# Refilling the expert ring in order, and gathering four channels two chunks later

## The chip, the cores and the metric

One NeuronCore of a Trainium2 chip runs the kernel. The metric is the device time of one execution in microseconds; lower is better.

## The reference

The kernel computes one layer of a hybrid decoder on 256 tokens of width 1024, in float32. The first half is `h = h + W_o(sum of three gated mixers of RMSNorm(h))` (sparse attention, causal pooling, short convolution). The second half, where the change lies, is a mixture of 32 experts in 4 groups of 8; each token goes to the two best experts of its best group:

```python
top_v, top_i = lax.top_k(e_in, EXPERT_TOP_K)              # best 2 of the 8 in the best group
top_w = jax.nn.softmax(top_v, axis=-1) * g_prob[tok, g_sel][:, None]
for e in range(N_EXPERTS):                                # w1, w3: 1024x256, w2: 256x1024
    h = jax.nn.silu(xt @ w1[e]) * (xt @ w3[e])
    out = out + combine[:, e:e + 1] * (h @ w2[e])
```

A final RMSNorm follows. The expert weights are 96 of the 132 MiB that the kernel reads, and every one is read once.

## The kernel before

**Blocks and chunks.** Experts are worked four at a time, as 8 blocks. An expert gets at most 32 tokens in a pass, so a block is 4 experts of 32 token places. The weights of a block come as 12 chunks of 1 MiB: 8 chunks `q` = 0 to 7 hold w1 and w3 for one eighth of the input channels (128) each, 4 chunks hold w2 for a quarter of the output columns each. A *round* is 4 blocks, 48 chunks (`NC`), numbered `c` = 0 to 47; there are two rounds in a pass, and with these inputs one pass.

**The ring.** Chunks land in 25 slots of 1 MiB (`ring`). `AT[c]` (line 78) is the slot of chunk c: 0 to 24 go to slots 0 to 24, chunk 25 to slot 0, chunks 26 to 47 to slots 2 to 23. Slots 1 and 24 thus hold one chunk in a round, the others two. `earlier(c)` is the chunk that held the slot before c: 25 back for chunk 25, 24 back for chunks 26 to 47. In the second round chunks 0 and 2 to 23 follow chunks that lie 23 and 24 back.

**SyncE's queue** issues every weight load, in chunk order. Chunks 0 to 23 are issued early, as slots come free from the first half of the layer (`early`, lines 551 to 625). Line 626 waits for `passes_done`, then line 627 loads chunk 24 (slot 24 held the router's constants and small tiles until then). Lines 629 to 631 load chunks 25 to 29 singly, 632 to 639 the rest of the round (two chunks in one transfer; the last one in halves), 643 to 664 the second round. Each of these first waits until TensorE has counted the slot's earlier chunk as used (`expert_used`).

**The router.** TensorE counts the tokens of each expert and signals `count_full` (line 1773). VectorE turns the counts into the number of passes in five small steps with the tile `pcnt`, and signals `passes_done` (lines 1330 to 1337). TensorE gathers channels 0 to 3 of block 0 (lines 1807 to 1813), then waits for `passes_done`, reads the number and enters the loop.

**TensorE in a block** (lines 1818 to 1906). `gather(k)` multiplies a slice of 128 channels of `h` with the 0/1 matrix `sel`, which leaves the block's tokens in PSUM bank 2. Channels 4 to 7 are gathered inside the block that uses them, 4 and 5 ahead of chunk q = 1, 6 and 7 ahead of q = 2. VectorE copies all four to `xgT`, with the norm's gain (line 1360, `xg1_done`); TensorE waits for that ahead of q = 4. After q = 2 come transposes of the weights of the block's tokens, from which VectorE makes `rslot`, `cmbT` and `share` (1364 to 1366, `cmb_done`) and then the next block's `sel` (1341). VectorE works in that order: 1360, 1364 to 1366, 1341, 1349. Channels 0 to 3 of the next block are gathered after q = 7 and between the second products; in the last block of a round (j = 3) they follow q = 4, 5, 6 and 7 one by one, each behind a wait for the next `sel` (1848 to 1850). Then come the second products (`second`) and the sums into the output banks (`combine`).

**After the last block** the sums are normed and stored by ScalarE, VectorE and SyncE. The tiles `fin`, `fing` and two of squares lie over ring slots 12 to 15.

Of the kernel before, what the change touches and what calls it, by code (L numbers as in the profile page):

```python
# [13 lines left out]
P = 128  # L14
D = 1024
T = 256
# [23 lines left out]
CAP = 32  # L40
EB = P // CAP
NB = NE // EB
EPS = 1e-6
NEG = -1e30
SLOT = 2048
SLOTS = 25

# [27 lines left out]
SLOT_XLO, SLOT_MERGED, SLOT_O, SLOT_XHI = 18, 19, 20, 21  # L75
SLOT_ATT, SLOT_Q, SLOT_ROUTER = 22, 23, 24

AT = [*range(SLOTS), 0, *range(2, SLOTS - 1)]
CHUNK_SET = {n: (SET_A, SET_B)[i % 2] for i, n in enumerate(SPLITS)}

NQ1 = KT
NQ2 = NQT
NQ = NQ1 + NQ2
ROUND = 4
NC = ROUND * NQ
ECHUNK = EB * 2 * HID
MAXPASS = T // CAP
# [4 lines left out]
def turn(c):  # L94

    return HELD[AT[c]].index(c)
# [15 lines left out]

K_ID = 0
K_IOTA = K_ID + P

K_TRI = K_IOTA + CAP
K_ONE = K_TRI + P
K_SL = K_ONE + P
K_RK = K_SL + HEADS
K_FOLD = K_RK + PER_GROUP  # L120
K_CAP = K_FOLD + 32
K_FOLD2 = K_CAP + MAXPASS
K_CB = K_FOLD2 + RC

K_DIST = K_CB + NT * HEADS * 16
# [9 lines left out]
def build(nc, x, params, consts, front, projs, small, wgrp, vecs, routerw, routerb, experts, out):  # L135
    with ExitStack() as ctx:
# [35 lines left out]
        def router(name, shape):  # L172

            t = over(name, shape, "ring", in_router[0])
            in_router[0] += math.prod(shape[1:])
            return t
# [3 lines left out]
        rb = router("rb", [P, RC])  # L180
        sPT1 = router("sPT1", [P, 3 * P])
        wg = router("wg", [P, 2, P])
        pcnt = router("pcnt", [P, 8 + MAXPASS])
        hidT = sb("hidT", [P, 4, KVG, 32])
        cw2 = sb("cw2", [P, 4, HD])
        kcT = over("kcT", [P, 32], "ring", SLOT_ATT * SLOT + 15 * P)
# [55 lines left out]

        routed = sb("routed", [P, 2, NT, NE])
        comb, rank = routed[:, 0], routed[:, 1]
        mask = over("mask", [P, NT, NE], "ring", in_router[0] - 8 - MAXPASS - 2 * P)[:]


        fin = over("fin", [P, NT, D], "ring", 12 * SLOT)
        fing = over("fing", [P, D], "ring", 13 * SLOT)
        last_squares = over("last_squares", [P, NT, D], "ring", 14 * SLOT)  # L250
        act_squares = over("act_squares", [P, NT, D], "ring", 15 * SLOT)
        xgT = kv[:].rearrange("p (k s) -> p k s", k=KT)
        yN, ylo = over("yN", [P, 2 * QC], "gab"), over("ylo", [P, 2 * QC], "gab", 2 * QC)
        gflat = gab[:].rearrange("p a c -> p (a c)")
# [7 lines left out]
        lg, gap1, key1, left, gap2, key2 = [kv[:, i * NT * RC:(i + 1) * NT * RC] for i in range(6)]  # L262
        first, second_of, both = [gflat[:, i * NT * RC:(i + 1) * NT * RC] for i in range(3)]
        top1, big1, top2, big2, behind, e2, weight, c1, c2, total = [vflat[:, 256 + 16 * i:256 + 16 * i + NT * ROWS] for i in range(10)]
        gexp = vflat[:, 416:432].rearrange("p (t e) -> p t e", t=NT)
        share1, share2 = [vflat[:, i * NT * NE:(i + 1) * NT * NE].rearrange("p (t e) -> p t e", t=NT) for i in range(2)]
        cmbT = over("cmbT", [P, T], "vbd")[:]
# [14 lines left out]
        rk8 = conr[:, K_RK - K_TRI:K_RK + PER_GROUP - K_TRI]  # L282
        fold = conr[:, K_FOLD - K_TRI:K_FOLD + 32 - K_TRI]
        fold2 = conr[:, K_FOLD2 - K_TRI:K_FOLD2 + RC - K_TRI]
        steps_of_cap = conr[:, K_CAP - K_TRI:K_CAP + MAXPASS - K_TRI]

# [213 lines left out]
        SCATTERED = (3, 5, 6, 7, 7)  # L502


        def summed(t, qt):

            c = t * QC if qt > 1 else qt * QC
            return bank[4 + t if qt < 2 else 4 + qt][:, c:c + QC]
# [9 lines left out]
        def _(sp):  # L518
# [104 lines left out]
            sp.wait_ge(wo_full, 4)  # L623
            early(SET_B + 2, SLOT_MERGED)
            early(SLOT_XHI, SLOT_ATT)
            sp.wait_ge(passes_done, 1)
            sp.dma_start(ring[:, SLOT_ROUTER], single(SLOT_ROUTER)).then_inc(router_slot_in, 16)

            for c in range(SLOTS, SLOTS + SINGLES):
                sp.wait_ge(expert_used, GIVEN + earlier(c) + 1)  # L630
                sp.dma_start(ring[:, AT[c]], single(c)).then_inc(expert_in[AT[c] // 2] if c % 2 else single_in, 16)
            for c in range(SLOTS + SINGLES, NC - 2, 2):
                sp.wait_ge(expert_used, GIVEN + earlier(c + 1) + 1)
                sp.dma_start(slots_of(c), experts[c // NQ, c % NQ // 2]).then_inc(expert_in[AT[c] // 2], 16)
            half = ECHUNK // 2
            for c, f, sem_in in ((NC - 2, slice(0, ECHUNK), expert_in[AT[NC - 2] // 2]), (NC - 1, slice(0, half), last_half_in),
                                 (NC - 1, slice(half, ECHUNK), last_in)):
                sp.wait_ge(expert_used, GIVEN + earlier(c) + 1)
                sp.dma_start(ring[:, AT[c], f], single(c)[:, f]).then_inc(sem_in, 16)
# [3 lines left out]
            with sp.Fori(1, passes * (NB // ROUND)) as r:  # L643
                def pair(c):

                    sp.wait_ge(expert_used, r * NC + (GIVEN + max(earlier(c), earlier(c + 1)) + 1))
                    sp.dma_start(slots_of(c), rounds[bass.ds(r % (NB // ROUND), 1), c // NQ, c % NQ // 2]  # L647
                                 .rearrange("o p c -> (o p) c")).then_inc(expert_in[AT[c] // 2], 16)

                for c in range(0, SLOT_ROUTER, 2):  # L650
                    pair(c)
                for c, sem_in in ((SLOT_ROUTER, router_slot_in), (SLOTS, expert_in[0])):
                    o = c % 2 * ECHUNK
                    sp.wait_ge(expert_used, r * NC + (GIVEN + earlier(c) + 1))
                    sp.dma_start(ring[:, AT[c]], rounds[bass.ds(r % (NB // ROUND), 1), c // NQ, c % NQ // 2, :, o:o + ECHUNK]
                                 .rearrange("o p c -> (o p) c")).then_inc(sem_in, 16)
                for c in range(SLOTS + 1, NC - 2, 2):
                    pair(c)
                for c, f, sem_in in ((NC - 2, slice(0, ECHUNK), expert_in[AT[NC - 2] // 2]), (NC - 1, slice(0, half), last_half_in),
                                     (NC - 1, slice(half, ECHUNK), last_in)):  # L660
                    sp.wait_ge(expert_used, r * NC + (GIVEN + earlier(c) + 1))
                    o = c % 2 * ECHUNK
                    sp.dma_start(ring[:, AT[c], f], rounds[bass.ds(r % (NB // ROUND), 1), c // NQ, c % NQ // 2, :, o + f.start:o + f.stop]
                                 .rearrange("o p c -> (o p) c")).then_inc(sem_in, 16)
# [765 lines left out]
        def _(pe):  # L1430
# [354 lines left out]
            def have_expert(bb, j, q):  # L1785

                c = j * NQ + q
                if SLOTS <= c < SLOTS + SINGLES and c % 2 == 0:
                    pe.wait_ge(single_in, 16 * (SINGLES // 2))
                if c == NC - 1:  # L1790
                    pe.wait_ge(last_in, bb * 16 + 16)
                elif c == SLOT_ROUTER:
                    pe.wait_ge(router_slot_in, bb * 16 + 16)
                else:
                    pe.wait_ge(expert_in[AT[c] // 2], bb * 32 + 16 * (turn(c) + 2))


            def gather(*ks):
# [7 lines left out]

            pe.wait_ge(sel_step, 1)
            for k in range(4):
                for t in range(NT):
                    ins = mm(bank[2 + k // 2][:, (k % 2) * P:(k % 2 + 1) * P], h[:, t, k * P:(k + 1) * P],  # L1810
                             flat(sel[:, t]), start=(t == 0), stop=(t == NT - 1))
                if k % 2:
                    ins.then_inc(xg_full, 1)

            pe.wait_ge(passes_done, 1)
            passes = pe.value_load(npass[0:1, 0:1], min_val=1, max_val=MAXPASS)

            def round_of_blocks(bb, last):

                for j in range(ROUND):  # L1820
                    b = bb * ROUND + j
                    pe.wait_ge(hn_done, b + 1)
                    for q in range(NQ1):
                        if q in (1, 2):
                            gather(2 * q + 2, 2 * q + 3)
                        if q == 0:
                            pe.wait_ge(xg0_done, b + 1)
                        if q == 2:
                            pe.wait_ge(xg1_done, b + 1)
                        if q == 4:  # L1830
                            pe.wait_ge(xg1_done, b + 2)
                        have_expert(bb, j, q)
                        for e in range(EB):
                            ins = mm(bank[0][CAP * e:CAP * (e + 1)], xgT[:, q, CAP * e:CAP * (e + 1)],  # L1834
                                     expert(j, q, e), start=(q == 0), stop=(q == NQ1 - 1))
                        if q == NQ1 - 1:
                            ins.then_inc(hid1_full, 1)
                        else:
                            ins.then_inc(expert_used, 1)
                        if q == 2:  # L1840
                            pe.wait_ge(sel_done, b + 1)
                            pe.wait_ge(hT_done, b + 1)
                            for t in range(NT):
                                nc.tensor.transpose(bank[1][:, t * P:(t + 1) * P], flat(selw[:, t]), ident)
                            for t in range(NT):
                                ins = mm(bank[1][:, T:T + 1], flat(sel[:, t]), stat[:, 26 + t:27 + t], start=(t == 0), stop=(t == NT - 1))
                            ins.then_inc(cmb_full, 1)
                        if j == ROUND - 1 and q >= 4:
                            pe.wait_ge(sel_step, b + 2)
                            gather(q - 4)  # L1850
# [184 lines left out]
```

## Time and profile before

| | us |
|---|---|
| median of 3 runs | 416.36 |
| lowest, highest | 415.26, 416.62 |
| the profiled execution | 415.54 |
| its span in the profile | 413.7 |

The span is what the profiler sees of the execution; 1.8 us lie around it. TensorE is busy for 382.1 us of the span (92%), VectorE for 198.4, ScalarE for 149.0. The DMA engines moved 139.89 MB. All times in the rows below are microseconds from the start of the span.

### The profile page before, as it was taken

Reading aid. Unit: us, or ns where it says so; the run is one execution under the profiler, and the core shown is the slowest. Engines: PE = TensorE matmul, PEld = TensorE weight load, DVE = VectorE, ACT = ScalarE, POOL = GpSimd, SP = SyncE. Lnnn points to the kernel's source line nnn. Section 1 sums busy time; section 2 is a strip of 40 time slices with the busy share of each in tenths; the row PEclk is TensorE's granted clock in tenths of the full one; section 3 lists DMA queues with packets and bytes.
Section 4 is the critical chain, followed back from the end, with each engine's and each line's share of the span. In section 5 each row is a group of like instructions: output and inputs, shape, how many; then the busy total and the mean of one; then the engine's idle time right before and its main releaser. Section 6 shows DMA issues by size and latency. Waiting matters only on the chain.

```text
span 413.7 us, 7503 instructions
## 1 busy us (share of the span) xinstructions
PE 382.1 (92%) x2990; PEld 265.2 (64%) x2990; DVE 198.4 (48%) x392; ACT 149.0 (36%) x283; POOL 12.2 (3%) x34
## 2 busy tenths in 40 slices
PE   7999999999999999999989999999899998688582
PEld 5999988767777777788865555555355544245241
DVE  3838693999898775784263121212122221211215
ACT  6834451638565635442221222222222222112023
POOL 3000000300000000000011000000000000000001
PEclk9999999999999999999999999999999999879996
DMA  7999999643441587569998999999999999999982
GB/s 299 412 412 358 395 390 365 265 152 101 154 147 67 196 329 281 184 243 398 420 418 321 394 428 429 426 414 430 426 425 428 426 417 429 428 428 428 425 335 103
DMA packets 17599, 139.89 MB, mean 338 GB/s; under 512 B 2336, under 2 KB 2720, under 8 KB 5792
## 3 DMA queue, kind: packets, MB, share of 16 engines
q1 hardware_dynamic: 16704, 138.60, 83.5%
q10 hardware_dynamic: 864, 0.84, 0.6%
q8 instruction: 24, 0.39, 0.4%
q14 instruction: 7, 0.06, 0.0%
HBM read 138.38 MB, written 1.05 MB: 337 GB/s over the span
## 4 chain that ended last, share of the span: by engine, by line
PE 73%; DMA 13%; DVE 6%; SPq 4%; ACT 2%; issue 2%; POOL 0%; POOLq 0%; DVEq 0%; ACTq 0%
DMA ring<-in_experts 12%; PE bank L1834 10%; PE bank L1802 6%; PE bank L1874 6%; PE bank L1596 5%; PE bank L1598 4%; PE bank L1597 4%; PE bank L1454 4%; PE bank L1455 4%; PE bank L1456 4%; SPq L647 4%; PE bank L1886 3%; PE bank L1718 2%; PE bank L1719 2%; PE bank L1717 2%
## 5 line engine op out<-in xcount | busy, mean ns | idle before, releaser
L1834 PE MATMUL bank<-ring,kv 128*32 128x512 f32 x512 | 65.7, 619 | 10.1 <-DMA ring<-in_experts 8.9
L481 DVE TENSOR_TENSOR part<-ring,part 128x2048 fp32r<-128x2048 f32 (+1 forms) x26 | 57.8, 2231 | 17.1 <-ACT part L474 17.1
L474 ACT CAST part<-ring 128x2048 fp32r<-128x2048 f32 (+1 forms) x26 | 48.0, 1847 | 29.5 <-DMA ring<-in_front 29.4
L1802 PEld LDWEIGHTS bank<-qcur,h 128*128 128x128 f32 x256 | 31.7, 191 | 28.2 <-issue 27.3
L1376 DVE SCALAR_TENSOR_TENSOR ylo<-bank,stat,yN 128x256 fp32r<-128x256 f32 (+1 forms) x40 | 17.1, 430 | 54.1 <-ACT yN L952 34.1
L1596 PE MATMUL bank<-part,xhi 128*128 128x512 f32 x96 | 39.2, 408 | 0.0
L1802 PE MATMUL bank<-qcur,h 128*128 128x128 f32 x256 | 39.1, 289 | 0.0
L1874 PE MATMUL bank<-ring,hidT 128*32 128x256 f32 (+1 forms) x640 | 35.2, 342 | 3.9 <-DMA ring<-in_experts 3.4
L1598 PE MATMUL bank<-part,xlo 128*128 128x512 f32 x96 | 37.6, 391 | 0.0
L1597 PE MATMUL bank<-part,xhi 128*128 128x512 f32 x96 | 37.5, 391 | 0.0
L1454 PE MATMUL bank<-xhi,part 128*128 128x256 f32 x128 | 36.6, 286 | 0.5 <-DVE xlo L1021 0.5
L1455 PE MATMUL bank<-xlo,part 128*128 128x256 f32 x128 | 36.2, 283 | 0.0
L1456 PE MATMUL bank<-xhi,part 128*128 128x256 f32 x128 | 36.2, 283 | 0.0
L1834 PEld LDWEIGHTS bank<-ring,kv 128*32 128x32 f32 x512 | 13.0, 110 | 32.0 <-issue 23.6
L952 ACT ACTIVATE yN<-bank,stat 128x256 fp32r<-128x256 f32 (+1 forms) x40 | 17.2, 431 | 42.3 <-PE bank L1874 42.3
L944 ACT ACT_TABLE_LOAD x7 | 9.0, 1283 | 50.6 <-DVE stat L1366 50.6
L1886 PE MATMUL bank<-yN,cmbT 128*128 128x256 f32 (+1 forms) x80 | 23.4, 318 | 2.8 <-DVE ylo L1376 2.5
L1454 PEld LDWEIGHTS bank<-xhi,part 128*128 128x128 f32 x128 | 24.5, 192 | 1.7 <-DVE xlo L1021 0.9
L1874 PEld LDWEIGHTS bank<-ring,hidT 128*32 128x32 f32 x640 | 16.6, 109 | 13.6 <-ACT hidT L946 3.1
L1455 PEld LDWEIGHTS bank<-xlo,part 128*128 128x128 f32 x128 | 24.6, 192 | 0.0
L1456 PEld LDWEIGHTS bank<-xhi,part 128*128 128x128 f32 x128 | 24.6, 192 | 0.0
L1360 DVE TENSOR_TENSOR kv<-bank,prm 128x512 f32<-128x512 f32 x8 | 5.5, 692 | 39.7 <-PE bank L1802 39.7
(251 smaller groups left out, 586.9 us busy)
## 6 DMA issues: line engine op xcount, KB each, us to landing
ring<-in_experts SPq DMA_DIRECT2D x30, 2048.0 KB, 33.5
ring<-in_experts SPq DMA_DIRECT2D x34, 1024.0 KB, 8.4
ring<-in_front SPq DMA_DIRECT2D x28, 1024.0 KB, 5.4
ring<-in_front SPq DMA_DIRECT2D x4, 512.0 KB, 6.8
ring<-in_projs SPq DMA_DIRECT2D x4, 512.0 KB, 5.2
ring<-in_experts SPq DMA_DIRECT2D x4, 512.0 KB, 32.5
ring<-in_front SPq DMA_DIRECT2D x2, 560.0 KB, 9.4
h<-in_x SPq DMA_DIRECT2D x2, 512.0 KB, 3.8
```

The lines of the kernel that those rows point to most:

```text
L474: nc.scalar.copy(high(n, half)[:, 0:c].bitcast(F32R), raw(n, half)[:, 0:c]).then_inc(hi_done, 1)
L481: nc.vector.tensor_tensor(low(n, half)[:, 0:c].bitcast(F32R), raw(n, half)[:, 0:c], high(n, half)[:, 0:c], ALU.subtract).then_inc(split_do ...
L1454: mm(dst, whi, ahi, start=start, stop=False)
L1455: mm(dst, whi, alo, start=False, stop=False)
L1456: return mm(dst, wlo, ahi, start=False, stop=stop)
L1596: mm(bank[t][:], XH[:, kk, cols], whi[:, k], start=(kk == 0), stop=False)
L1597: mm(bank[t][:], XH[:, kk, cols], wlo[:, k], start=False, stop=False)
L1598: ins = mm(bank[t][:], XL[:, kk, cols], whi[:, k], start=False, stop=(kk == KT - 1))
L1802: ins = mm(bank[2][:, (k % 4) * P:(k % 4 + 1) * P], h[:, t, k * P:(k + 1) * P], flat(sel[:, t]), start=(t == 0), stop=(t == NT - 1))
L1834: ins = mm(bank[0][CAP * e:CAP * (e + 1)], xgT[:, q, CAP * e:CAP * (e + 1)], expert(j, q, e), start=(q == 0), stop=(q == NQ1 - 1))
L1874: ins = mm(second_out(p, slice(CAP * e, CAP * (e + 1))), hT[:, ht, CAP * e:CAP * (e + 1)], second_weights(j, p, ht, e), start=(ht == 0), s ...
L1886: mm(sum_of_piece(t, p), onehot, yN[:, place(p)].bitcast(F32R), start=False, stop=False)
```

## The change

It does four things.

1. Chunks 25 to 47 take slots 0 to 22 in order. Every one of them now follows a chunk 25 back. In the second round chunks 0 to 22 follow chunks 23 back, and 23 and 24 have slots that held one chunk. The semaphores of arrival are renumbered (`arrival`). A pair of the second round waits for the later of its two.
2. Chunk 24's load waits for `count_full` in place of `passes_done`. `pcnt` and the constants `K_CAP` leave slot 24; `fin` and its companions move down by one slot.
3. Channels 4 and 5 are gathered ahead of q = 3, channels 6 and 7 ahead of q = 4.
4. TensorE waits for `passes_done` and reads the number ahead of its gather of channel 3, in place of after it.

```diff
-AT = [*range(SLOTS), 0, *range(2, SLOTS - 1)]
+AT = [*range(SLOTS), *range(ROUND * NQ - SLOTS)]
...
-        pcnt = router("pcnt", [P, 8 + MAXPASS])
+        pcnt = vflat[:, 432:440 + MAXPASS]
...
-        fin = over("fin", [P, NT, D], "ring", 12 * SLOT)
+        fin = over("fin", [P, NT, D], "ring", 11 * SLOT)
...
-        steps_of_cap = conr[:, K_CAP - K_TRI:K_CAP + MAXPASS - K_TRI]
+        steps_of_cap = con[:, K_CAP:K_CAP + MAXPASS]
...
+        def arrival(c):
+            return expert_in[c % SLOT_ROUTER // 2]
...
-            sp.wait_ge(passes_done, 1)
+            sp.wait_ge(count_full, 1)
             sp.dma_start(ring[:, SLOT_ROUTER], single(SLOT_ROUTER)).then_inc(router_slot_in, 16)
...
-                sp.dma_start(ring[:, AT[c]], single(c)).then_inc(expert_in[AT[c] // 2] if c % 2 else single_in, 16)
+                sp.dma_start(ring[:, AT[c]], single(c)).then_inc(arrival(c) if c % 2 else single_in, 16)
...
             for k in range(4):
+                if k == 3:
+                    pe.wait_ge(passes_done, 1)
+                    passes = pe.value_load(npass[0:1, 0:1], min_val=1, max_val=MAXPASS)
                 for t in range(NT):
...
-            pe.wait_ge(passes_done, 1)
-            passes = pe.value_load(npass[0:1, 0:1], min_val=1, max_val=MAXPASS)
...
-                        if q in (1, 2):
-                            gather(2 * q + 2, 2 * q + 3)
+                        if q in (3, 4):
+                            gather(2 * q - 2, 2 * q - 1)
```

## Rows read from the trace of the kernel before

**Rows 1.** The page, what the DMA engines moved in 40 slices of 10.34 us.

```profile
GB/s 299 412 412 358 395 390 365 265 152 101 154 147 67 196 329 281 184 243 398 420 418 321 394 428 429 426 414 430 426 425 428 426 417 429 428 428 428 425 335 103
```

**Rows 2.** The chain that ended last, 150 to 414: start, us, what.

```profile
348.27 49.81 DMA ring<-in_experts
398.21 1.10 PE bank L1874 x16
```

**Rows 3.** Stretches: from:to, us, TensorE's granted clock, DMA share, GB/s.

```profile
212.00:218.00 6.00, 1.00 1.01 422
218.00:221.00 3.00, 1.00 0.88 279
...
224.50:227.50 3.00, 1.00 0.75 243
227.50:234.00 6.50, 1.00 0.95 369
218.00:234.00 16.00, 1.00 0.91 335
264.00:396.00 132.00, 0.97 1.01 425
```

**Rows 4.** SyncE's timeline, chunks 24, 25 and 26: start, us, line.

```profile
218.03 0.33 SPq L627 DMA_DIRECT2D ring<-in_experts  x1
...
220.43 0.33 SPq L631 DMA_DIRECT2D ring<-in_experts  x1
...
224.60 0.33 SPq L631 DMA_DIRECT2D ring<-in_experts  x1
```

**Rows 5.** Timeline from 211 to 226, router and block 0: start, us, engine, line.

```profile
216.28 0.61 PE L1772 MATMUL bank<-mask,conr 128*128 128x32 f32 x4
...
217.83 0.18 DVE L1337 CAST npass<-pcnt 128x2 int32<-128x2 f32 x1
...
223.58 0.69 DVE L1360 TENSOR_TENSOR kv<-bank,prm 128x512 f32<-128x512 f32 x1 [3.59 <-PE bank L1802]
```

**Rows 6.** TensorE's read of the pass count: ns min/median/max, start.

```profile
L1816 PEldq TENSOR_LOAD <-npass x1: 490/490/490, 218.0 to 218.0; - x1
```

**Rows 7.** The chain, 150 to 414, where it runs along TensorE: start, us, what.

```profile
216.95 2.05 PE bank L1810 x16
219.31 1.07 PE bank L1834 x8
220.37 1.09 PE bank L1802 x8
...
282.41 1.07 PE bank L1834 x8
...
305.16 1.06 PE bank L1834 x8
```

**Rows 8.** Timeline of blocks 6 and 7: start, us, idle before and releaser.

```profile
363.37 1.93 PE L1834 MATMUL bank<-ring,kv 128*32 128x512 f32 x8 [2.01 <-DMA ring<-in_experts]
...
378.41 1.07 PE L1834 MATMUL bank<-ring,kv 128*32 128x512 f32 x8
...
383.07 1.06 PE L1834 MATMUL bank<-ring,kv 128*32 128x512 f32 x8 [0.43 <-DMA ring<-in_experts]
...
384.89 0.16 DVE L1364 COPY stat<-bank 128x1 f32<-128x1 f32 x1 [1.51 <-PE bank L1846]
...
385.84 0.42 DVE L1341 TENSOR_TENSOR qcur<-con,routed 128x256 f32<-128x256 f32 x1
...
388.39 1.07 PE L1834 MATMUL bank<-ring,kv 128*32 128x512 f32 x8 [2.55 <-DMA ring<-in_experts]
...
393.20 1.06 PE L1834 MATMUL bank<-ring,kv 128*32 128x512 f32 x8 [1.46 <-DMA ring<-in_experts]
```

**Rows 9.** Stretches of blocks 6 and 7: busy times, then granted clock, DMA share, GB/s.

```profile
360.00:364.00 4.00, 1.99 (x12) 0.20 (x8) 0.00 (x0) 0.00 (x0) 0.00 (x0) 0.50 0.99 422
...
384.00:388.00 4.00, 1.84 (x18) 0.85 (x14) 1.77 (x6) 0.00 (x0) 0.00 (x0) 1.00 0.99 422
```

More of the change, by code:

```diff
@@ L44 @@
 NEG = -1e30
+NQ1 = KT
+NQ2 = NQT
+NQ = NQ1 + NQ2
+ROUND = 4
 SLOT = 2048
@@ L76 @@
 SLOT_ATT, SLOT_Q, SLOT_ROUTER = 22, 23, 24
-AT = [*range(SLOTS), 0, *range(2, SLOTS - 1)]
+AT = [*range(SLOTS), *range(ROUND * NQ - SLOTS)]
 CHUNK_SET = {n: (SET_A, SET_B)[i % 2] for i, n in enumerate(SPLITS)}
[L83 to L86, printed above, removed]
 NC = ROUND * NQ
@@ L114 @@
 K_IOTA = K_ID + P
-K_TRI = K_IOTA + CAP
+K_CAP = K_IOTA + CAP
+K_TRI = K_CAP + T // CAP
 K_ONE = K_TRI + P
@@ L120 @@
 K_FOLD = K_RK + PER_GROUP
-K_CAP = K_FOLD + 32
-K_FOLD2 = K_CAP + MAXPASS
+K_FOLD2 = K_FOLD + 32
 K_CB = K_FOLD2 + RC
@@ L244, in build @@
         comb, rank = routed[:, 0], routed[:, 1]
-        mask = over("mask", [P, NT, NE], "ring", in_router[0] - 8 - MAXPASS - 2 * P)[:]
-        fin = over("fin", [P, NT, D], "ring", 12 * SLOT)
-        fing = over("fing", [P, D], "ring", 13 * SLOT)
-        last_squares = over("last_squares", [P, NT, D], "ring", 14 * SLOT)
-        act_squares = over("act_squares", [P, NT, D], "ring", 15 * SLOT)
+        mask = over("mask", [P, NT, NE], "ring", in_router[0] - 2 * P)[:]
+        fin = over("fin", [P, NT, D], "ring", 11 * SLOT)
+        fing = over("fing", [P, D], "ring", 12 * SLOT)
+        last_squares = over("last_squares", [P, NT, D], "ring", 13 * SLOT)
+        act_squares = over("act_squares", [P, NT, D], "ring", 14 * SLOT)
         xgT = kv[:].rearrange("p (k s) -> p k s", k=KT)
@@ L630, in _ @@
                 sp.wait_ge(expert_used, GIVEN + earlier(c) + 1)
-                sp.dma_start(ring[:, AT[c]], single(c)).then_inc(expert_in[AT[c] // 2] if c % 2 else single_in, 16)
+                sp.dma_start(ring[:, AT[c]], single(c)).then_inc(arrival(c) if c % 2 else single_in, 16)
             for c in range(SLOTS + SINGLES, NC - 2, 2):
                 sp.wait_ge(expert_used, GIVEN + earlier(c + 1) + 1)
-                sp.dma_start(slots_of(c), experts[c // NQ, c % NQ // 2]).then_inc(expert_in[AT[c] // 2], 16)
+                sp.dma_start(slots_of(c), experts[c // NQ, c % NQ // 2]).then_inc(arrival(c), 16)
             half = ECHUNK // 2
-            for c, f, sem_in in ((NC - 2, slice(0, ECHUNK), expert_in[AT[NC - 2] // 2]), (NC - 1, slice(0, half), last_half_in),
+            for c, f, sem_in in ((NC - 2, slice(0, ECHUNK), arrival(NC - 2)), (NC - 1, slice(0, half), last_half_in),
                                  (NC - 1, slice(half, ECHUNK), last_in)):
@@ L647, in pair @@
                     sp.dma_start(slots_of(c), rounds[bass.ds(r % (NB // ROUND), 1), c // NQ, c % NQ // 2]
-                                 .rearrange("o p c -> (o p) c")).then_inc(expert_in[AT[c] // 2], 16)
+                                 .rearrange("o p c -> (o p) c")).then_inc(arrival(c), 16)
                 for c in range(0, SLOT_ROUTER, 2):
                     pair(c)
-                for c, sem_in in ((SLOT_ROUTER, router_slot_in), (SLOTS, expert_in[0])):
+                for c, sem_in in ((SLOT_ROUTER, router_slot_in), (SLOTS, arrival(SLOTS))):
                     o = c % 2 * ECHUNK
@@ L658, in _ @@
                     pair(c)
-                for c, f, sem_in in ((NC - 2, slice(0, ECHUNK), expert_in[AT[NC - 2] // 2]), (NC - 1, slice(0, half), last_half_in),
+                for c, f, sem_in in ((NC - 2, slice(0, ECHUNK), arrival(NC - 2)), (NC - 1, slice(0, half), last_half_in),
                                      (NC - 1, slice(half, ECHUNK), last_in)):
@@ L1794, in have_expert @@
                 else:
-                    pe.wait_ge(expert_in[AT[c] // 2], bb * 32 + 16 * (turn(c) + 2))
+                    pe.wait_ge(arrival(c), bb * 32 + 16 * (turn(c) + 2))
             def gather(*ks):
```

## The prediction, made before the changed kernel was run

> **What bounds the kernel now.** I read the chain that ended last first. Its late part is one transfer of expert weights: issued at 348.27, landed 49.81 us later, and within 0.2 us of the landing TensorE starts the products that needed it [rows 2]. So the weights' arrival sets the end, and the last 8 us or so of work hang on it. A transfer that is 50 us under way says that the queue is deep. Next the page's row of GB/s: from the slice that starts at 238 us on it is flat near 425, up to the last two slices [rows 1]; over 264 to 396 it is 425 [rows 3]. In that stretch nothing on an engine can make the weights come earlier; the reader should look for what is lost before it. The row shows a dip of 321 in the slice from 217 to 227 us, between 418 and 394 [rows 1]. In narrower stretches: 422 up to 218, then 279, later 243, then 369 until 234; over 218 to 234 the mean is 335 [rows 3]. That is (1 - 335/425) x 16 = 3.4 us of lost transfer time. Every us of it that is won back brings all later weights 1 us earlier, as long as TensorE keeps up.
>
> Two holes make most of it. The first, (1 - 279/425) x 3 = 1.0 us, is around chunk 24: SyncE issues it at 218.03, as soon as the pass count is written at 218.01 [rows 4, 5], and the earlier transfers run out at about 218.5. The second, (1 - 243/425) x 3 = 1.3 us, is around chunk 26: chunk 25 is issued at 220.43, when q = 0 of block 0 ends, and chunk 26 only at 224.60 [rows 4], since its slot is that of chunk 2, and the two pairs of gathers stand ahead of chunk 2. After 227.5 another (1 - 369/425) x 6.5 = 0.9 us is lost while single chunks trickle out.
>
> **The change part by part.** The sum is made against the profiled execution, 415.54 us, which is 0.8 under the median of 416.36; I give the result for both.
>
> *Chunk 24.* `count_full` comes with the end of the count's products, 216.28 + 0.61 = 216.89, the pass count at 217.83 + 0.18 = 218.01 [rows 5]: 1.1 us earlier, while the DMA engines still run at 422 [rows 3]. The first hole closes. But chunk 24 then moves from about 218.5 to 221.0 (1.05 MB at 425 GB/s is 2.5 us), and chunk 25 still waits for q = 0 of block 0.
>
> *The read of the pass count.* It took 0.49 us on TensorE's queue, from 218.0 on, while the array was busy with gathers until 219.0 [rows 6, 7]. Ahead of channel 3 it finds fewer products in front of it (three quarters of 2.05 us, done at 218.5), so that gather starts some 0.3 us late; what then follows it, the loop's entry, is partly behind the gather. Between 0 and 0.5 us on the start of block 0, I take 0.2. So chunk 25 is issued at about 220.6, close to the end of chunk 24's data. In the second hole the issue at 224.60 came about as late against the end of the data as this one would, or slightly later: I take 0.9 of its 1.3 us for the new hole at chunk 25 (bounds 0.3 and 1.3).
>
> *Chunks 26 to 29.* Chunk 26 follows chunk 1 now, and no gather stands ahead of q = 1. With 1.0 us for a chunk of products (219.31 to 220.37) and 1.1 for a pair of gathers [rows 7], q = 1 ends at 221.5 and q = 2 at 222.5: chunks 26 and 27 are issued then, 3.1 us and more ahead of 224.60. The second hole goes. Chunk 28 follows q = 3, which has the transposes (0.7) and the gather of channels 4 and 5 ahead: about 225.3. Chunk 29 follows q = 4, at about 228.4. By then 5 chunks of 2.5 us have been issued, enough until 234. Of the 0.9 us lost after 227.5 I take half as won (bounds none and all).
>
> *Sum for the weights.* Lost before 3.4. Lost after: 0.9 at chunk 25, 0.4 to 0.5 later, together 1.4. Gain 2.0 us. Highest: all 3.4. Lowest: the second hole goes (1.3), the first (1.0) goes, and a full hole of 1.3 opens at chunk 25: 1.0.
>
> The Trainium skill (DMA: Bandwidth & Descriptors, section Anatomy of one DMA) puts a fixed 2.0 us on a transfer, mostly the wait for the receipt of the last byte, which the next transfer in a queue does not pay. It gives it for GpSimd's queue. By it a late chunk costs the engines less than 2 us, and the two holes of 1.0 and 1.3 agree.
>
> *The gathers' place in the block.* Nothing is added: 16 products of 128 x 128 and VectorE's copy of 0.69 us [rows 5] stand as before. But the copy's cover goes. Before, q = 2, the transposes and q = 3 lay between gathers and wait, over 2.7 us; now the gather of 6 and 7 is directly followed by the wait. VectorE's copy of block 0 starts at 223.58, within 0.1 of the end of the gathers (two chunks at 1.07 and 1.0 and two gathers at 1.1, from 219.31 [rows 7]); it takes 0.69, and I give the answer another 0.1: 0.9 us a block, 8 blocks, 7.2 us of TensorE. Bounds: 0.7 (the copy alone) and 1.5. In the last block of a round the wait for the next `sel` after q = 4 comes on top: VectorE needs 384.89 to 386.26 = 1.4 us from `rslot` to `sel` [rows 8], and q = 4 covers 1.0: 0.4 more. The SiLU's wait for `cmb_done` stays covered by q = 5 to 7 (3 us).
>
> *Does TensorE keep up?* Before, three blocks took 282.41 - 219.31 = 63.1 and the fourth 22.7 [rows 7], and the weights caught up with TensorE in block 5 to 7. Blocks with 0.9 more, the fourth with 1.3, start from 219.5: block 4 at 309.4, block 5 at 331.3, block 6 at 353.2, block 7 at 375.1. Block 7 began at 378.41 before [rows 8], held by weights; 2.0 us earlier is 376.4. So TensorE is 1.3 us ahead even there. In block 7, with weights 2.0 earlier: q = 2 at 381.1 (383.07 before), transposes done at 382.8, gather, q = 3 and gather until 386.0, wait 0.9, q = 4 at 386.9 (its weights come at 386.4), the wait for `sel` until 388.1, gather, q = 5, gather until 390.4; the weights of q = 6 come at 391.2 (393.20 before). From there all is as before, 2.0 us earlier. The 7.2 us lie in waits for weights, among them 2.55, 2.01 and 1.46 [rows 8]; the thinnest cover is this 0.8 us.
>
> *Order of the slots later on.* A chunk of the second round waits for one chunk more of use, some 2 us, and for TensorE's lag of 3 to 8 us. Against this stands a queue of up to 50 us [rows 2]. Nothing. Renumbered semaphores, the moved tiles and constants: same instructions, nothing.
>
> **Forecast:** 415.54 - 2.0 = 413.5 for the profiled execution, 414.4 beside the median.
>
> **The rivals.**
> A, the hole only moves: the engines stand idle at chunk 25 as long as at 24 and 26, or block 0 starts 0.5 later. Gain 0.3 to 1.2 us, about 415.5. For it: chunk 25's issue hangs on q = 0 alone. Against: chunk 24's issue moves less than the hole at 26 was wide.
> B, all is won: 3.0 to 3.4 us, about 413.1. Chunk 25 would have to be issued while 24 flows well.
> C, the clock falls late. In block 6 the granted clock was 0.50, the 1.2 GHz level, from 360 to 364, around a wait of 2.01 us, and 8 products took 1.93 us in place of 1.06 [rows 8, 9]; this was covered by waits for weights. In block 7 it stayed at 1.00, though TensorE was busy for 1.84 of 4 us [rows 9]. The change moves the gathers out of the wait ahead of q = 2 of block 7, so that TensorE idles some 2.7 us there. If the clock then is at the lower level over the last 7 us, which nothing covers, half of them is lost: +3.5 - 2.0 = +1.5, about 417.9. It decides if the drop reaches past the landing of the last pair.
> The Trainium skill (TensorE: Matmul & The Clock Gate, Part 1) says that the gate goes by how busy the array has been; these rows fit it in block 6 and leave block 7 open.
> D, the gather's wait becomes the bound: if it costs x a block, the cover of 1.3 + 2.7 us up to q = 2 of block 7 is gone at x = 1.5, the gain at x = 1.75, and from 1.9 the kernel is slower by over 0.3%; at 2.2 it would be at 420. Against: VectorE has nothing else to do there.
> E, no effect: the weights are bound somewhere that I don't see. 416.4.
>
> **The numbers.** What can be told from no change is 0.3%, 1.25 us. Forecast 0.53 (own range 413.8 to 415.1), B 0.05: faster 0.58. A 0.25, E 0.05: same 0.30. C 0.07, D 0.05: slower 0.12. The range goes from B's lower end, 416.4 - 3.4 = 413.0, to 416.6, 0.2 above E.
>
> **What would show it.** After the change: chunk 24 issued near 217.0, 26 and 27 before 223; 218 to 234 at 385 to 395 GB/s in place of 335; the chain still on a transfer, landing near 396; eight waits of TensorE of about 0.9 us behind line 1360. It is wrong if the last landing has not moved, if the chain's end runs along TensorE from block to block, or if the clock is below 1 after 390.

## The result and the profile after

The changed kernel took 412.56 us in the median of 8 executions (411.73 to 414.75), the kernel before 415.56 (8 executions, 415.24 to 416.62). The ratio is 0.9934, 95% interval 0.9909 to 0.9959: 2.7 us less. The profiled execution took 412.76 us (span 411.0) against 415.54: 2.8 less. Among the 8 executions, three took 414.46 to 414.75, the others 411.73 to 412.76. I had forecast 2.0 less and, from a median of 416.36 over three executions of the kernel before, the range 413.0 to 416.6. The time is below it.

The stretches of the changed kernel (from:to, us, granted clock, DMA share, GB/s), to be read beside [rows 3]:

```profile
218.00:221.00 3.00, 1.00 0.99 391
221.00:224.50 3.50, 1.00 0.86 286
224.50:227.50 3.00, 1.00 1.01 429
227.50:234.00 6.50, 1.00 1.01 426
218.00:234.00 16.00, 1.00 0.97 389
...
264.00:378.00 114.00, 1.00 1.01 428
```

The holes at chunks 24 and 26 and the thin supply after 227.5 have gone, one hole at chunk 25 has come. Over 218 to 234 the mean is 389 in place of 335. The last row is the surprise: over 264 to 378 the rate is 428. The kernel before, in the same stretch:

```profile
264.00:378.00 114.00, 0.97 1.01 425
```

SyncE's timeline in block 0, chunks 24 to 28 (start, us, line), beside [rows 4]:

```profile
217.10 0.33 SPq L632 DMA_DIRECT2D ring<-in_experts  x1
...
220.85 0.33 SPq L636 DMA_DIRECT2D ring<-in_experts  x1
...
221.71 0.33 SPq L636 DMA_DIRECT2D ring<-in_experts  x1
...
222.57 0.33 SPq L636 DMA_DIRECT2D ring<-in_experts  x1
...
225.27 0.33 SPq L636 DMA_DIRECT2D ring<-in_experts  x1
```

TensorE's waits from 180 us on (who waited for whom: us in total, times, longest):

```profile
PE bank L1839 <- DVE kv L1365: 6.3, 8, 0.8
...
PE bank L1839 <- DMA ring<-in_experts: 2.8, 1, 2.8
```

Line 1365 is VectorE's copy of channels 4 to 7 (1360 before). Its eight waits are there, 0.8 us each. In their place the waits for weights ahead of the first products have shrunk to one, of 2.8 us. That one is in block 7, and the chain that ended last goes through it (start, us, what):

```profile
332.83 46.68 DMA ring<-in_experts
...
379.64 1.06 PE bank L1839 x8
```

The weights of q = 2 of block 7 land 3.4 us earlier (383.07 in [rows 8], 379.64 here). But behind them the chain runs along TensorE, and no later transfer of weights is on it. TensorE's timeline shows why (start, us, line, idle before):

```profile
374.95 1.92 PE L1839 MATMUL bank<-ring,kv 128*32 128x512 f32 x16
379.64 1.06 PE L1839 MATMUL bank<-ring,kv 128*32 128x512 f32 x8 [2.77 <-DMA ring<-in_experts]
...
381.28 2.03 PE L1807 MATMUL bank<-qcur,h 128*128 128x128 f32 x8
383.23 1.78 PE L1839 MATMUL bank<-ring,kv 128*32 128x512 f32 x8
384.95 1.16 PE L1807 MATMUL bank<-qcur,h 128*128 128x128 f32 x8
386.89 1.07 PE L1839 MATMUL bank<-ring,kv 128*32 128x512 f32 x8 [0.78 <-DVE kv L1365]
```

After the idle 2.77 us a pair of gathers takes 2.03 us instead of 1.16 and the products of q = 3 take 1.78 instead of 1.07: the clock is at its lower level. The same in the stretches (busy times, granted clock, DMA share, GB/s):

```profile
380.00:384.00 4.00, 4.00 (x26) 2.57 (x22) 0.00 (x0) 0.00 (x0) 0.00 (x0) 0.67 1.02 434
384.00:388.00 4.00, 3.17 (x24) 1.12 (x16) 1.82 (x6) 0.00 (x0) 0.00 (x0) 0.91 0.99 422
```

So two things differed from my account: the weights gained 3.4 us, not 2.0, and 0.6 us of that (3.4 - 2.8) was lost again in block 7.

### The profile page after: what moved, and what is told of

It is laid out like the page before. It is cut to its first block, busy times and chain, and to the rows that moved or that the text cites. A ratio compares the mean times of both kernels' runs of the same rounds, so it can differ in the third digit from the quotient of the medians.

```text
span 411.0 us, 7504 instructions
## 1 busy us (share of the span) xinstructions
PE 379.0 (92%) x2990; PEld 265.8 (65%) x2990; DVE 197.1 (48%) x392; ACT 149.0 (36%) x283; POOL 13.1 (3%) x34
## 4 chain that ended last, share of the span: by engine, by line
PE 75%; DMA 12%; DVE 7%; ACT 2%; issue 2%; POOL 0%; POOLq 0%; SPq 0%; DVEq 0%; ACTq 0%
DMA ring<-in_experts 11%; PE bank L1839 11%; PE bank L1807 6%; PE bank L1879 6%; PE bank L1601 5%; PE bank L1602 4%; PE bank L1603 4%; PE bank L1459 4%; PE bank L1460 4%; PE bank L1461 4%; PE bank L1891 3%; PE bank L1722 2%; PE bank L1724 2%; PE bank L1723 2%; PE bank L1563 1%
## 5 line engine op out<-in xcount | busy, mean ns | idle before, releaser
L1839 PE MATMUL bank<-ring,kv 128*32 128x512 f32 x512 | 62.1, 604 | 10.0 <-DVE kv L1365 6.3
L1807 PEld LDWEIGHTS bank<-qcur,h 128*128 128x128 f32 x256 | 32.6, 195 | 21.9 <-issue 19.9
L1839 PEld LDWEIGHTS bank<-ring,kv 128*32 128x32 f32 x512 | 14.1, 109 | 34.5 <-issue 24.2
```

Source lines behind the costliest of these rows:

```text
L1807: ins = mm(bank[2][:, (k % 4) * P:(k % 4 + 1) * P], h[:, t, k * P:(k + 1) * P], flat(sel[:, t]), start=(t == 0), stop=(t == NT - 1))
```

## The experiments

The theory at the start: the gain is the closed holes in block 0; the gathers' place costs TensorE 0.8 to 0.9 us a block, covered until block 7, where the clock can fall. The rival: the gathers' place is what makes the gain, or the order of the slots raises the flat rate. All ratios are against the kernel before in the same series, whose median was 415.4 to 415.9. "Less" or "slower" beside a ratio is worked out from it; where two changed kernels are compared, it is by their medians.

**e1**, the changed kernel with the gathers back:

```diff
-                        if q in (3, 4):
-                            gather(2 * q - 2, 2 * q - 1)
+                        if q in (1, 2):
+                            gather(2 * q + 2, 2 * q + 3)
```

> The changed kernel with the gathers of channels 4 to 7 back ahead of q = 1 and 2; slots in order, chunk 24 at the count and the early read stay. Theory 1 (the gain is the weights' holes in block 0; the gathers' new place costs TensorE 0.9 us a block, hidden up to block 7, and there an idle stretch of 2.8 us ahead of q = 2 after which the clock falls in some executions): chunk 26 is issued about 1 us later than in the changed kernel, at 222.9, still in time, so the holes stay as small (218 to 234 near 385 GB/s). No wait behind the copy of channels 4 to 7, no long idle stretch ahead of q = 2 of the last block: 411.5 to 412.5 us, ratio to before 0.991 to 0.993, all executions together, none at 414.5. Theory 2 (the gathers' move is what brings chunks 26 to 28 early enough): 218 to 234 falls back to about 360 GB/s and the time is 414 or more.

412.84 us, ratio 0.9931 (0.9918 to 0.9945), five executions within 412.49 to 413.32. The rate over 218 to 234 was 360, which is what the second theory had said, but its time (414 or more) was not. So the gathers' move does help the weights, by (389 - 360)/428 x 16 = 1.1 us. Of the changed kernel's 11 executions (3 of them in e14 below), the five with a mean clock of 0.995 (median 411.85) are 1.0 us below e1's median and the five with 0.985 or 0.986 (median 414.49) 1.6 above, so in the mean over all of them nothing is left of the gain. No execution of e1 was near 414.5.

**e2**, gathers back in blocks 3 and 7 alone:

```diff
-                        if q in (3, 4):
+                        if j == ROUND - 1 and q in (1, 2):
+                            gather(2 * q + 2, 2 * q + 3)
+                        if j < ROUND - 1 and q in (3, 4):
                             gather(2 * q - 2, 2 * q - 1)
```

> The changed kernel, but in the last block of each round (blocks 3 and 7) the gathers stand ahead of q = 1 and 2 as before; in the other six blocks they stay ahead of q = 3 and 4. Theory 1 (in block 7 TensorE idles ahead of q = 2 and in some executions runs at the lower clock afterwards, with nothing to cover it): that idle stretch is filled with 2.2 us of gathers, the clock stays at 1.00 from 380 on, and the executions near 414.5 go: all at 411 to 412.5, ratio 0.990 to 0.992. Theory 2 (the spread from 411.7 to 414.7 comes from somewhere else, such as the front of the kernel): the same two groups of times as in the changed kernel.

412.07 us, ratio 0.9912 (0.9898 to 0.9925), all five within 411.62 to 412.64. The group near 414.5 is gone, as theory 1 said; the chain ends on the landing of the last pair again. One number of mine was wrong: the clock did not stay at 1.00. In e2's profile it was 1.00 over 380 to 384 and fell behind the next wait, the 2.08 us ahead of q = 4 (busy times, granted clock, DMA share, GB/s; then TensorE):

```profile
384.00:388.00 4.00, 2.94 (x12) 1.16 (x12) 0.00 (x0) 0.00 (x0) 0.00 (x0) 0.58 0.99 422
```

```profile
385.06 1.94 PE L1841 MATMUL bank<-ring,kv 128*32 128x512 f32 x8 [2.08 <-DMA ring<-in_experts]
```

There it cost nothing: TensorE still waited for the last weights afterwards. Filling the wait ahead of q = 2 thus did not keep the clock up to the end, it moved the fall to a place where it is covered.

**e3**, slots in order and nothing else (the diff of `AT`, `arrival` and the moved `fin`, on the kernel before):

> The kernel before with slots 0 to 22 refilled in order, and nothing else of the change: chunk 24 still waits for the pass count, gathers ahead of q = 1 and 2. Theory 1: chunk 26 is issued when q = 1 ends, at about 222.5 in place of 224.6, and chunks 27 to 31 one chunk of use earlier; the hole at chunk 24 (1.0 us) stays, the one at chunk 26 (1.3 us) and most of the 0.9 us behind it go: 2.0 us less, about 413.6, ratio 0.995. Rival (the order of the slots raises the flat rate after 264 from 424 to 428 GB/s, which is worth another 1 us): ratio 0.993, and 427 or more GB/s over 264 to 378.

414.44 us, ratio 0.9971 (0.9959 to 0.9983): 1.2 us less. 218 to 234 at 373 GB/s, from 264 at 425. The order of the slots closes holes ((373 - 335)/425 x 16 = 1.4 us) and does not touch the flat rate.

**e4**, chunk 24 at the count and nothing else (on the kernel before, with `pcnt` and `K_CAP` moved; the cut shows two places of the edit):

```diff
-K_TRI = K_IOTA + CAP
+K_CAP = K_IOTA + CAP
+K_TRI = K_CAP + T // CAP
...
-            sp.wait_ge(passes_done, 1)
+            sp.wait_ge(count_full, 1)
             sp.dma_start(ring[:, SLOT_ROUTER], single(SLOT_ROUTER)).then_inc(router_slot_in, 16)
```

> The kernel before with chunk 24 issued at the count of tokens instead of at the pass count (and the tile and constants that this needs moved out of its slot), and nothing else of the change. Theory 1: chunk 24 is issued at 217.0, the hole around 219 closes, but the next hole opens at chunk 25 (issued at 220.4, when chunk 24's data ends at 221) and the one at chunk 26 stays: gain 0.1 to 0.6 us, ratio 0.9985 to 1.0. Rival (each hole stands for itself and closing one is worth its 1.0 us): ratio 0.9975. The flat rate after 264 stays at 424 to 426 GB/s, if that rate belongs to the slots' order; if it differs from run to run by itself, it can be anything from 424 to 430.

413.87 us, ratio 0.9954 (0.9941 to 0.9968): 1.9 us less, beyond both. The holes were as theory 1 said, moved and not closed (333 GB/s over 218 to 234, 335 before), but the flat rate was 429:

```profile
264.00:378.00 114.00, 0.99 1.01 429
```

So something in this edit raises the flat rate, and that one chunk is issued 0.9 us earlier is hardly a reason for it 50 us later. The other candidate is an address, which e5 and e6 test by itself: `K_CAP` makes the tile `con` 32 bytes longer, and the ring, allocated behind it, starts at byte 9472 of each partition instead of 9440 (worked out from the sizes of the tiles ahead of it).

**e5 and e6**, the ring moved by 32 bytes, with the same edit on two kernels. On the kernel before it moves the ring to 9472, on e2's to 9504:

```diff
+        npass = sb("npass", [P, 2], I32)
         ring = sb("ring", [P, SLOTS, SLOT])
...
-        npass = sb("npass", [P, 2], I32)
```

> The kernel before with one small tile (npass, 32 bytes a partition) allocated ahead of the ring instead of behind it; nothing else. The ring then starts at byte 9472 of each partition, as in the changed kernel, in place of 9440; 9472 is a multiple of 64, 9440 is not. Theory 1 (the moved constants lengthened the tile ahead of the ring by 32 bytes, and with the ring's rows on multiples of 64 bytes the weights land about 1% faster; this is what chunk 24's edit gained beyond its hole): the flat rate over 264 to 378 rises from 424 to 428 or more GB/s, 233 MB of weights behind 218 us take 1.0 to 2.0 us less: 413.6 to 414.5, ratio 0.9955 to 0.9975. Theory 2 (the earlier issue of chunk 24 is worth 1.7 us by itself): ratio 0.999 to 1.001, flat rate 424 to 426.

> The kernel of e2 (changed kernel, gathers of blocks 3 and 7 ahead of q = 1 and 2) with npass allocated ahead of the ring: the same edit as in e5, but here it moves the ring from byte 9472, a multiple of 64, to 9504, which is none. Theory 1 (the ring's start sets the flat rate): the rate over 264 to 378 falls from 428 to 431 back to 424 to 426, the time rises by 1.0 to 2.0 us over e2's 412.07, to 413.1 to 414.1. Theory 2 (it is chunk 24's issue): 412.0 as e2.

e5: 413.98 us, ratio 0.9959 (0.9945 to 0.9974), 1.7 us less than before with the holes untouched (330 GB/s over 218 to 234). e6: 413.49, ratio 0.9948 (0.9933 to 0.9962), 1.4 us more than e2. The stretch from 264 to 378, e5 first, then e6:

```profile
264.00:378.00 114.00, 0.99 1.01 429
```

```profile
264.00:378.00 114.00, 1.00 1.01 425
```

**e7**, e2's kernel with channels 4 to 7 gathered together ahead of q = 3 in the six other blocks:

```diff
-                        if j < ROUND - 1 and q in (3, 4):
-                            gather(2 * q - 2, 2 * q - 1)
+                        if j < ROUND - 1 and q == 3:
+                            gather(4, 5, 6, 7)
```

> The kernel of e2, but in the six blocks that are not last in a round all four channels 4 to 7 are gathered together ahead of q = 3, so that q = 3 covers VectorE's copy. Theory 1 (e2 is bound by the landing of weights up to block 7, the copy's 0.9 us a block are hidden there): the eight waits of TensorE behind the copy fall to none, 5 us of TensorE come free, and the time stays within 0.3 us of e2's 412.07; chunk 28 is issued 1.1 us later, at 226.4, which opens no hole. Theory 2 (TensorE's 0.9 us a block still cost something): 411.5 or less.

411.88 us, ratio 0.9911 (0.9896 to 0.9926), as e2. TensorE's products no longer wait for the copy: e2's six waits of 0.8 us, 4.7 us in sum, are gone. The time set free brings nothing here, since the chain still ends on a landing of weights (at 393.92).

**e8**, the gathers moved on the kernel before (the diff of the change, that part alone), and **e11**, the same kernel again:

> The kernel before with the gathers of channels 4 to 7 ahead of q = 3 and 4, and nothing else of the change. Chunk 26 (it follows chunk 2 here) is issued when q = 2 ends, at about 222.4 in place of 224.6, chunk 27 near 225.1 in place of 226.3. Theory 1 (the hole at chunk 26 is worth its 1.3 us, whichever edit closes it, and the ring's start is as before, so no more): the hole at 24 stays, 218 to 234 rises from 335 to about 370 GB/s, the flat rate stays at 424 to 426: 414.0 to 414.5, with some executions 1 to 3 us later, where the clock falls after the idle stretch ahead of q = 2 of block 7. Rival (TensorE's 7.2 us in 8 blocks outweigh the gain): 416 or more.

> The kernel of e8 once more, for a profile: in e8 the two executions with a mean clock of 0.995 took 414.7 and the ten with 0.983 to 0.987 took 415.7 to 417.6, and the profile there is one of the two. Theory: in the slower ones the granted clock is at the lower level for some us after TensorE's wait ahead of q = 2 of block 7, the gathers and products of q = 3 and 4 take nearly twice as long, and the chain runs along TensorE from there to the end. Rival: the clock falls in block 6 or in the front of the kernel, and the time is lost elsewhere.

e8: 416.68 us, 12 executions, ratio 1.0025 (1.0011 to 1.0038): slower by 1.0 us, although 218 to 234 rose to 366 GB/s. Two executions had a mean clock of 0.995 and took 414.7; ten had 0.983 to 0.987 and took 415.7 to 417.6. Theory 1 had expected the group near 414.7 as the rule and the later one as the exception; it was the other way round. The rival named the time, but its mechanism (TensorE's 7.2 us outweigh the gain) would have cost time in all executions, and the two at 414.7 gained 0.9 us. e11 was like those two (414.43, clock 0.995), so no profile shows one of the ten; that the clock in block 7 is the cause there too is inferred from the mean clocks and from e14.

**e14**, the changed kernel again, shows in its profile one of the executions near 414.5:

> The changed kernel once more, for its profile. Theory: if its mean clock is 0.985 to 0.986, the time is near 414.5, the clock is at the lower level for 5 us or more after TensorE's wait ahead of q = 2 of block 7, and the chain runs along TensorE from there. If it is 0.995, the time is near 411.8 and the clock stays at 1.00 in block 7. Rival: the clock is down elsewhere in a slow one.

414.23, 412.19 and 414.49 us, at mean clocks 0.986, 0.995 and 0.986. The profile is of the first. Its stretches, and TensorE's timeline in block 7:

```profile
380.00:384.00 4.00, 4.00 (x26) 3.14 (x22) 0.00 (x0) 0.00 (x0) 0.00 (x0) 0.57 1.03 438
384.00:388.00 4.00, 3.57 (x16) 1.78 (x8) 0.39 (x1) 0.00 (x0) 0.00 (x0) 0.57 0.99 422
```

```profile
379.51 1.07 PE L1839 MATMUL bank<-ring,kv 128*32 128x512 f32 x8 [2.65 <-DMA ring<-in_experts]
...
381.69 2.06 PE L1807 MATMUL bank<-qcur,h 128*128 128x128 f32 x8
383.67 1.94 PE L1839 MATMUL bank<-ring,kv 128*32 128x512 f32 x8
385.54 2.04 PE L1807 MATMUL bank<-qcur,h 128*128 128x128 f32 x8
388.36 1.06 PE L1839 MATMUL bank<-ring,kv 128*32 128x512 f32 x8 [0.78 <-DVE kv L1365]
```

Nearly the same wait, the weights of q = 2 at nearly the same time (379.51 and 379.64), and q = 4 at 388.36 in place of 386.89: the transposes, two pairs of gathers and one chunk at about half speed. In e11's profile, whose execution kept its clock but for the first products behind the wait, q = 2 to q = 4 took 5.8 us (382.41 to 388.23):

```profile
382.41 1.25 PE L1834 MATMUL bank<-ring,kv 128*32 128x512 f32 x8 [2.74 <-DMA ring<-in_experts]
...
388.23 1.07 PE L1834 MATMUL bank<-ring,kv 128*32 128x512 f32 x8 [0.78 <-DVE kv L1360]
...
392.13 1.07 PE L1834 MATMUL bank<-ring,kv 128*32 128x512 f32 x8 [0.27 <-DMA ring<-in_experts]
```

In the profile of the changed kernel it took 7.25 us (379.64 to 386.89), in e14 8.85 (379.51 to 388.36): 1.4 and 3.0 lost. The last row says more: with the clock up, TensorE reached q = 6 ahead of its weights even with the gathers in their new place, by 0.27 us. Of the changed kernel's 11 executions, five had a mean clock of 0.995 and took 411.73 to 412.35, one 0.989 and 412.76, five 0.985 or 0.986 and 414.23 to 414.75.

**e10**, e7's kernel with the read of the pass count behind the gather of channel 3:

```diff
-                if k == 3:
-                    pe.wait_ge(passes_done, 1)
-                    passes = pe.value_load(npass[0:1, 0:1], min_val=1, max_val=MAXPASS)
...
+            pe.wait_ge(passes_done, 1)
+            passes = pe.value_load(npass[0:1, 0:1], min_val=1, max_val=MAXPASS)
```

> The kernel of e7 with TensorE's read of the pass count behind the gather of channel 3 again, as in the kernel before. Theory (ahead of channel 3 the read costs TensorE 0.35 us in the gathers, and q = 0 starts at 219.6 to 219.8 in place of 219.3, so chunk 25 is issued 0.3 to 0.5 us late): chunk 25 is issued near 220.5, the hole at it shrinks by 0.3 to 0.5 us, the time by as much: 411.4 to 411.6, ratio 0.990. Rival (the place of the read is worth nothing, the hole at chunk 25 hangs on the count of transfers in flight): 411.9.

411.54 us, ratio 0.9903 (0.9888 to 0.9918); the best kernel, 4.0 us under the kernel before. Chunk 25 was issued at 220.62, 0.1 ahead of e7, and 218 to 234 had 395 GB/s in place of 386. The 0.3 us against e7 are as expected, but the intervals overlap and q = 0 started only 0.1 us earlier (219.50 in place of 219.61), so they are not shown to come from the read.

**e9, e12 and e13**, which starts are fast. e9 is e7 with `stat` (192 bytes) ahead of the ring; e12 is e10 with the ring directly behind `h`, ahead of `con` and `prm`; e13 is e10 with `qcur` (1024 bytes) ahead of the ring.

```diff
+        qcur = sb("qcur", [P, T])
         ring = sb("ring", [P, SLOTS, SLOT])
```

> The kernel of e7 with the small tile stat (192 bytes a partition) allocated ahead of the ring. The ring starts at byte 9664 in place of 9472: still a multiple of 64, no longer one of 128. If a start on 64 bytes is what the flat rate wants: 428 to 430 GB/s over 264 to 378 and 411.9 as e7. If it wants 128 or more: 424 to 426, and 1.0 to 2.0 us more, 412.9 to 413.9.

> The kernel of e10 with the ring allocated directly behind h, ahead of con and prm. The ring starts at byte 8576: a multiple of 128 but not of 256 (9472, the fast start so far, is a multiple of both; 9440, 9504 and 9664, the slow ones, of neither). If a start on 128 bytes is enough: 428 to 430 GB/s over 264 to 378 and 411.5 as e10. If it takes 256: 424 to 426, and 412.9 to 413.5.

> The kernel of e10 with the tile qcur (1024 bytes a partition) allocated ahead of the ring. The ring starts at byte 10496, a multiple of 256 like 9472. If a start on 256 bytes is what counts: 428 GB/s or more over 264 to 378 and 411.5 as e10 (ratio 0.990). If it was that one address: 424 to 426 and 413 (ratio 0.994).

| start of the ring | remainder by 256 | GB/s, 264 to 378 | kernels |
|---|---|---|---|
| 9440 | 224 | 425 | before, e3, e8 |
| 9472 | 0 | 428, 429 | after, e1, e2, e4, e5, e7, e10 |
| 9504 | 32 | 425 | e6 |
| 9664 | 192 | 426 | e9: 413.47 us, e7 has 411.88 |
| 8576 | 128 | 426 | e12: 413.01 us, e10 has 411.54 |
| 10496 | 0 | 429 | e13: 411.63 us |

The last two rows, e12 and then e13, in their profiles:

```profile
264.00:378.00 114.00, 0.97 1.01 426
```

```profile
264.00:378.00 114.00, 0.97 1.01 429
```

Both multiples of 256 are fast, the four other starts are not; 64 and 128 are not enough. Between e7 and e9 only two allocations change places, and in e12 and e13 one tile moves, so neither the order of the work nor its amount can be the reason. The two fast starts lie 1024 bytes apart (both leave 256 by 512 and by 1024): that a coarser grid than 256 is what counts was not tested. Ratios: e9 0.9951 (0.9938 to 0.9963), e12 0.9939 (0.9925 to 0.9952), e13 0.9900 (0.9883 to 0.9916).

## Why the prediction was wrong, step by step

*What bounds the kernel.* Right: the weights' arrival set the end before, and the transfer time lost between 218 and 234 could be won.

*The sum for the weights' holes.* Right in sum, 2.0 forecast, (389/428 - 335/425) x 16 = 1.9 measured. That it fits so closely is luck, for two of its terms were off in opposite directions: chunk 25's hole is 1.4 us ((1 - 286/428) x 3.5 + (1 - 391/428) x 3), forecast 0.9, and nothing was lost after 227.5, where I had kept 0.4 to 0.5. Chunk 25 was issued at 220.85, not 220.6, because q = 0 started at 219.73, not 219.5: the read of the pass count cost the 0.2 us that I had put down for it, but the gathers ahead of it began 0.2 later than before (217.14, 216.95 before). With the issue at 220.62 (e10) the hole is still 1.2 us, so the rest is the size of the term. The issues of chunks 24, 26, 27, 28 and 29 came within 0.2 us of what I had worked out. In parts: the slots' order alone won 1.4 us of transfer time (e3), the gathers' move 1.1 in its presence (e1), chunk 24's issue alone nothing (e4): here closing the first hole of a series only moved it.

*The step that failed:* "Renumbered semaphores, the moved tiles and constants: same instructions, nothing." The moved constants lengthened a tile by 32 bytes and with it brought the ring to a multiple of 256 bytes. That is worth 1.4 to 1.7 us (e5, e6, e9, e12), about half of the whole gain, and it has no sign in the instructions. With it the weights come 3.4 us earlier at q = 2 of block 7 in place of 2.0. The other part of the miss is the anchor: three executions of the kernel before gave a median of 416.36, eight gave 415.56, and my lower end of 413.0 stood on the first. On 415.56 it would have been 412.2, and the measured 412.56 would have lain inside the range for a wrong reason.

*Rival B*, all is won, 3.0 to 3.4 us, has the size that was measured in the medians (3.0), by coincidence: its condition, that chunk 25 is issued while 24 flows well, did not hold, and 1.4 us of hole stayed.

*The gathers' place.* Right: 0.8 us a block measured, 0.9 forecast, and covered up to block 7, which began at 374.95 (forecast 375.1). Earlier weights did not make the cover of 0.8 us at q = 6 too thin: behind the wait ahead of q = 2 TensorE's work starts with the weights and moves with them, and in e11, at full clock, 0.27 us were left over. What it could not cover was the clock: 1.4 us lost against the 0.8 of cover that I had worked out agree with the 0.6 us that the profiled execution gave back. So my sign "the chain still on a transfer, landing near 396" did not come in it: the chain ended along TensorE.

*Rival C.* I gave the late fall of the clock 0.07. The two profiles of the changed kernel show it in the place I had named, behind the idle stretch ahead of q = 2 of block 7 (forecast 2.7 us, measured 2.77 and 2.65), for a short while in one and for up to 7 us in e14. By the mean clocks it came in full in 5 of 11 executions and in part in the profiled one. It costs up to 3.0 us of TensorE; the group near 414.5 took 2.6 us more than the one near 411.9, by the medians. I had priced it as falling in the last 7 us; it falls just behind the wait, and the clock is back before the end. It fits that the kernels on the fast ring start with those gathers ahead of q = 1 and 2 of block 7 have no group near 414.5 (e1, e2 and e7 with five executions each, e10 and e13 with four each), though in the profiles of all but e1 the clock falls too, two chunks later. On the kernel before the same edit costs more than it brings (e8). Why the clock falls in some executions and not in others is open.

*Rivals A, D and E.* A's mechanism was real for chunk 24's part (e4), not for the whole. D and E did not happen.

## What to carry to other kernels

Before pricing an edit at nothing, look at what it does to the addresses of the tiles allocated behind it; here a DMA-bound stretch won 0.9% (429 GB/s against 425) by the ring's start. When holes in a transfer stream follow each other, ask which one opens when the first is closed. Work that fills a wait on TensorE near the end of a kernel is worth keeping there even if its place looks free: without it a fall of the clock can come where little covers it (e14), with it the fall came later and was covered (e2). A copy of 0.7 us can be covered from another place (e7).

## What the runs showed of the hardware

Over 264 to 378 the weights arrived at 428 to 429 GB/s with the destination's start on a multiple of 256 bytes, at 425 to 426 with remainders 32, 128, 192 and 224. Most of these transfers carry a pair of chunks, 16 KiB per partition. The Trainium skill (DMA: Bandwidth & Descriptors, section How a descriptor splits into AXI transactions) says that a transaction of up to 256 bytes, in beats of 32, must start from a 256-byte boundary, so that a piece of data that starts off the boundary has its first transaction start below it. The section speaks of what a transaction reads; here only the place where the bytes are written was varied. If the same held for it, a row of 16 KiB would take 64 transactions and 512 beats from a boundary, 65 and 513 from 32 bytes behind one, 65 and 519 from 224 behind; these are estimates from that section. The residue 256 agrees with e12 and e13. That e6 (32) and the kernel before (224) are alike, 425 both, fits the count of transactions better than that of beats. The loss is 0.9%, less than the 1.6% that one transaction more in 64 would give. The mechanism is not shown.

TensorE's granted clock fell from the 2.4 GHz level to the 1.2 GHz level behind a wait of 2.65 to 2.77 us that followed 1.92 us of products, and in e14 was down for up to 7 us while the array had work all the time. The length of the wait alone does not decide it: behind waits of 2.74 and 2.75 us in e11 and e8 only the first products were slowed (1.25 us in place of 1.07), a stretch of 2.55 us idle in the same block of the kernel before left the clock at 1.00 [rows 9], and behind nearly equal waits ahead of q = 4 it was 0.58 over 384 to 388 in e2 (2.08 us) and 1.00 in e1 (2.10 us).
